# Splitting POOL's weight subtraction into two halves, and PE's wait with it

## The reference, cut to what matters

```
h = h + hgrn2_mixer(rmsnorm(h, ...), w_q, w_f, w_i, w_g, g_norm, w_o, lb)
h = h + sq_relu_mlp(rmsnorm(h, ...), w_up, w_down)      # square(relu(x @ up)) @ down
k_nope, k_rope, v = shared_mla_kv(h, ...)
h = h + mla_mixer(rmsnorm(h, ...), ...)                 # softmax attention
...
x = x + merged @ w_out ; x = x + (silu(gate) * val) @ w_ffn_down
```

## Time and profile before

| | |
|---|---|
| median of 3 runs | 2708.05 us (2705.83 to 2711.03) |
| the profiled execution, its own time | 2706.62 us |
| its span, first to last instruction | 2704.7 us |
| PE busy | 2563.7 us (95%) |
| POOL busy | 1135.5 us (42%) |
| DVE busy | 1494.2 us (55%) |
| mean granted TensorE clock | 0.984 |

### The profile page before, as it was taken

The page is one execution under the profiler, slowest core; times in us unless marked ns, Lnnn a source line. Parts: engine busy times, 40 slices in busy tenths (PEclk is TensorE's granted clock), DMA queues, the critical chain, the costliest instruction groups (busy, mean ns, idle before and its releaser), DMA issues.

```text
span 2704.7 us, 31079 instructions
## 1 busy us (share of the span) xinstructions
PE 2563.7 (95%) x11716; PEld 2038.7 (75%) x11716; DVE 1494.2 (55%) x2034; ACT 673.1 (25%) x1319; POOL 1135.5 (42%) x764
## 2 busy tenths in 40 slices
PE   8999899999978999999999999999989998899998
PEld 6888688888757768888887677777766667688886
DVE  4764565465666634645657674444445787555511
ACT  2003521021324431200213213333322431222200
POOL 3333255555522125555554353333322224455554
PEclk9999899999989999999999999999999999899999
DMA  6334366565522126656654474454454435456655
GB/s 202 125 110 141 101 192 196 189 197 190 187 78 78 63 79 193 195 188 198 206 188 154 145 240 152 158 166 143 154 192 145 135 111 180 151 191 194 195 188 170
DMA packets 149049, 436.62 MB, mean 161 GB/s; under 512 B 14064, under 2 KB 18352, under 8 KB 148912
## 3 DMA queue, kind: packets, MB, share of 16 engines
q1 hardware_dynamic: 64224, 200.29, 25.0%
q0 software_dynamic: 67584, 201.35, 21.3%
q10 hardware_dynamic: 17104, 33.14, 3.6%
HBM read 417.90 MB, written 16.83 MB: 161 GB/s over the span
## 4 chain that ended last, share of the span: by engine, by line
issue 35%; PE 34%; POOL 24%; DVE 3%; DMA 2%; ACT 1%; DVEq 1%; ACTq 0%; POOLq 0%; SPq 0%
POOL w_lo L471 19%; PE bank L523 9%; PE bank L525 9%; PE bank L526 9%; POOL w_hi L453 5%; PE bank L730 2%; DMA projections<-spill_out 1%; PE bank L1157 1%; PE bank L1166 1%; PE bank L804 1%; PE bank L807 0%; PE bank L806 0%; DMA residual<-x_in 0%; PE bank L1124 0%; DVE next_gained L2376 0%
## 5 line engine op out<-in xcount | busy, mean ns | idle before, releaser
L471 POOL TENSOR_TENSOR w_lo<-w_raw,w_hi 128x1024 fp32r<-128x1024 f32 x376 | 903.0, 2402 | 14.5 <-DMA w_hi<-stream 6.4
L453 POOL DMA_DIRECT2D w_hi<-stream x376 | 226.3, 602 | 1537.1 <-PE bank L523 1349.2
L523 PE MATMUL bank<-x_hi,w_hi 128*128 128x512 f32 x1464 | 588.9, 402 | 27.6 <-POOL w_lo L471 14.7
L525 PE MATMUL bank<-x_lo,w_hi 128*128 128x512 f32 x1464 | 574.3, 392 | 0.0
L526 PE MATMUL bank<-x_hi,w_lo 128*128 128x512 f32 x1464 | 573.8, 392 | 0.0
L523 PEld LDWEIGHTS bank<-x_hi,w_hi 128*128 128x128 f32 x1464 | 277.3, 189 | 113.2 <-issue 40.0
L526 PEld LDWEIGHTS bank<-x_hi,w_lo 128*128 128x128 f32 x1464 | 277.2, 189 | 59.2
L525 PEld LDWEIGHTS bank<-x_lo,w_hi 128*128 128x128 f32 x1464 | 277.7, 190 | 56.0 <-issue 2.4
L2084 DVE TENSOR_TENSOR relu_sq<-relu 128x512 f32<-128x512 f32 x64 | 178.7, 2792 | 94.4 <-ACT relu L1459 94.4
L526 PE MATMUL bank<-hidden_hi,w_lo 128*128 128x512 f32 x512 | 199.2, 389 | 0.0
L525 PE MATMUL bank<-hidden_lo,w_hi 128*128 128x512 f32 x512 | 199.2, 389 | 0.0
(11 more groups left out here) (447 smaller groups left out, 4488.2 us busy)
## 6 DMA issues: line engine op xcount, KB each, us to landing
w_hi<-stream POOLq DMA_DIRECT2D x376, 512.0 KB, 4.8
w_raw<-stream SPq DMA_DIRECT2D x376, 512.0 KB, 3.7
projections<-spill_out ACTq DMA_DIRECT2D x56, 256.0 KB, 2.1
ssm_x<-projections ACTq DMA_DIRECT2D x4, 1024.0 KB, 7.1
gate_tiles<-projections ACTq DMA_DIRECT2D x16, 256.0 KB, 2.8
ssm_z<-projections ACTq DMA_DIRECT2D x16, 256.0 KB, 2.6
residual<-x_in SPq DMA_DIRECT2D x4, 512.0 KB, 10.5
toeplitz_hi<-toeplitz_rows_hi POOLq DMA_DIRECT2D x4, 512.0 KB, 6.4
```

The lines of the kernel that those rows point to most:

```text
L453: e.dma_start(in_slot(whi, t % SLOTS, o), in_stream(o)).then_inc(hi_ready[t % SLOTS], 16)
L471: e.tensor_tensor(wlo[:, s, :], raw[:, s, :], whi[:, s, :].bitcast(F32), ALU.subtract).then_inc(lo_ready, 1)
L523: mm = e.matmul(out, wh, rh, start=first, stop=False)
L525: e.matmul(out, wh, rl, start=False, stop=False)
```

## The change

POOL subtracts each tile in two instructions of 512 columns, blocks 0 to 3 and then blocks 4 to 7, and raises the semaphore after each. The semaphore is counted in halves. PE waits at block 0 for the first half and at block 4 for the second. The signal that frees a slot is still given once a tile. `Reader.tile` now waits for both halves before its first matmul.

```
-        lo_ready = sem("lo_ready")
+        lo_ready = sem("lo_half_ready")
...
-                e.tensor_tensor(wlo[:, s, :], raw[:, s, :], whi[:, s, :].bitcast(F32),
-                                ALU.subtract).then_inc(lo_ready, 1)
+                for half in range(2):
+                    cut = slice(512 * half, 512 * half + 512)
+                    e.tensor_tensor(wlo[:, s, cut], raw[:, s, cut], whi[:, s, cut].bitcast(F32),
+                                    ALU.subtract).then_inc(lo_ready, 1)
...
-                    if b == 0:
-                        tile = pos[0] // BLK
-
-                        e.wait_ge(lo_ready, (tile + 1) if i is None else stride * i + (tile + 1))
-                        self.fresh = True
+                    if b % (BLK // 2) == 0:
+                        half = pos[0] // (BLK // 2)
+
+                        e.wait_ge(lo_ready, (half + 1) if i is None else 2 * stride * i + (half + 1))
+                        self.fresh = self.fresh or b == 0
```

## The result

The changed kernel takes 2719.89 us (median of 20 runs, 2716.33 to 2723.91) and the kernel before, run beside it, 2712.51 us (20 runs, 2705.57 to 2719.86). The ratio is 1.0026, 95% interval [1.0018, 1.0035]: slower by 0.26%, just past the 0.2% that a measurement here can tell. I had forecast 2706.4 us, a ratio of 0.9994, "within 0.2%" as the likeliest and 2714 as the top of the range. The time missed the range. A third of the distance is bad luck with the base: the forecast stood on a median of three runs, 2708.05, and twenty runs of the same kernel gave 2712.51, 4.5 us more. The rest, 9.0 us, is the change itself: forecast 1.6 us faster, measured 7.4 us slower. Three executions on record, one of the kernel before (3577.41 us), one of changed_filled (3731.10) and one of dense_split_filled (5206.77), ran over 30% longer than the others and are left out of every comparison.

A forecast was written before the change was run, and what follows sets the result against it. PE was taken as the bound, busy 95% of the span, so only its 141 us standing still could pay. 2706.62 - 4.7 + 3.0 = 2704.9 profiled, 2706.4 for the runs; the likeliest case's range was 2701 to 2714.

The forecast's parts named there:

- Cost of one half: POOL's subtraction: first half ready after 1.30 us, 1.10 earlier than now; two halves near 2.55.
- e: Extra POOL time of a split tile over a whole subtraction: taken as 0.15 us, between 0 and 0.52.
- f: Fixed part of one POOL subtraction: taken as 0.20 us, between the zero end and DVE's share of 0.33.
- Rival 2: POOL's fixed part is large, so 20 holds each cost more: about 2715 us; chance 0.10 with a reverse shift of holds.
- The late tiles: PE's starts on two latent-stage and three dense-stage tiles come earlier: gains 1.10 + 1.09 and 1.59 us.
- The first tile: At the kernel's start PE begins up to 1.05 us earlier; 0.9 counted as gain.
- PE's added waits: Some 370 new waits at block 4 cost nothing; uncovered, up to 3.7 us.
- POOL's queue: The cast now stands behind two subtractions; POOL's 2.46 us idle in dense stages covers the extra time.
- DVE beside the subtraction: POOL keeps the port through both halves, so 20 DVE holds on PE's path end 0.15 later: 3.0 us lost.
- rival 1: DVE gets in between POOL's halves, shortening holds in attention: 18.2 us gained there, about 2685 us; chance 0.25.
- Each hold costs e: Each of 20 DVE holds on PE's path ends 0.15 us later, 3.0 us in all.
- rival 3: Earlier starts shift attention's subtractions so fewer hold `mla_probs`, up to 1.8 us each: 2702 us or less; chance 0.07.

The follow-up runs named there:

- changed_filled: Changed kernel plus four unread PE matmuls ahead of the wait in each of nine latent-attention stalls: 2711.60 us, ratio 1.0002 to the kernel before.
- dense_split_filled: Kernel before with only dense-stage tiles split, PE waiting by halves, and four unread matmuls in each of nine latent-attention stalls: 2706.66 us, 0.9981.
- waits_filled: Kernel before with PE waiting by halves on a whole subtraction, plus four unread matmuls in each of nine latent-attention stalls: 2710.34 us, 1.0000.
- before_filled: Kernel before plus four unread PE matmuls in each of nine latent-attention stalls: 2708.65 us, 0.9998.
- second_half_after_block4: Changed kernel, but POOL subtracts a tile's second half only once PE has run the previous tile's first block-4 matmul: 2702.45 us, 0.9961 to the kernel before.
- section 5: Changed kernel splitting only dense-stage, attention or four latent-stage tiles, or all but the latent attention's: 1.0016, 1.0020, 0.9991, 1.0018 to the kernel before.
- runs 1 and 2: Kernel before with only PE's waits by halves (2712.37 us, 1.0011), then with only POOL's split and one signal after the second half (2724.07 us, 1.0062).
- split_in_attention_only: Changed kernel splitting only the tiles of the latent attention, sparse attention and state space, others subtracted whole: 2717.03 us, 1.0020 to the kernel before.
- late_tiles_only: Changed kernel splitting only the five tiles PE had waited for behind the first, others subtracted whole: 2710.27 us, 1.0003 to the kernel before.
- split_in_dense_stages: Changed kernel splitting only tiles of the MLPs, latent products and FFN from its fourth tile, others whole: 2714.14 us, 1.0016 to the kernel before.
- quarters: Changed kernel with four subtractions of 256 columns a tile, signals after the second and fourth: 2725.13 us, 1.0055 to the kernel before.

## Why the prediction was wrong, point by point

- **Cost of one half.** Right. Predicted 1.30 for one and 2.55 for two, measured 1.296 and 2.54. So e is 0.14, f 0.19, and the value between zero and the proportional share taken from DVE's rows was a good choice; DVE's 14% itself would have given 0.33. Rival 2, a large fixed part, is out.
- **The late tiles.** Right. The waits for `w_lo` fell to the first tile's. Predicted 1.10 + 1.09 + 1.59 = 3.8; measured from start to start 1.09 and 1.08 in the latent stage, 0.37, 0.92 and 0.65 in the dense ones, 4.1 in all.
- **The first tile.** The gain of 0.9 isn't shown. I counted it because the next subtraction moves forward as well. The first matmul did start 1.41 after POOL's first subtraction instead of 2.48. But the pieces hold DVE's instructions for the first tile too:

```profile
14.50 1.38 POOL L473 TENSOR_TENSOR w_lo<-w_raw,w_hi 128x512 fp32r<-128x512 f32 x1
...
14.66 1.76 DVE L1939 TENSOR_TENSOR x_lo<-x_gained,x_hi 128x512 fp32r<-128x512 f32 x1
...
15.84 1.72 POOL L473 TENSOR_TENSOR w_lo<-w_raw,w_hi 128x512 fp32r<-128x512 f32 x1
...
16.48 0.80 PE L525 MATMUL bank<-x_hi,w_hi 128*128 128x512 f32 x1 [0.43 <-DVE x_lo L1939]
17.07 0.63 PE L527 MATMUL bank<-x_lo,w_hi 128*128 128x512 f32 x1
...
17.76 0.68 DVE L1939 TENSOR_TENSOR x_lo<-x_gained,x_hi 128x512 fp32r<-128x512 f32 x1
...
18.49 0.79 PE L525 MATMUL bank<-x_hi,w_hi 128*128 128x512 f32 x1 [0.37 <-DVE x_lo L1939]
```

  `x_lo` takes 1.76 beside the subtraction and 0.68 without, and PE waits three times, 1.07 in all, where it had waited once for 0.99. On the clock of the span the tile ends 0.9 later than before, but the loads had also landed later: POOL's first subtraction began at 11.10 instead of 9.94. In the nine profiles with the first tile whole PE's 97th matmul starts between 41.3 and 44.1 us, in the eight with it split between 41.5 and 44.0. Neither a gain nor a loss can be told from that.
- **PE's added waits.** Right at nothing: 204.45 us for the same 900 matmuls with and without them. waits_filled differs from before_filled by 0.0002, with intervals of 0.0014 to either side.
- **POOL's queue.** Right. The cast goes out on time; POOL's idle time before it fell from 2.46 to 2.31, by e.
- **DVE beside the subtraction, and rival 1.** Right where it mattered, not everywhere. `relu_sq` measured 3.46 (predicted 3.47), the waits at L1006 21.1 (predicted 21). All 137 DVE instructions of the profiled run that stood held when a first half began stayed held through the second. Of 37 held ones that came during the first half, 29 were held through and eight got in at the seam, as rival 1 has it. The `x_lo` above is one: it ends at 16.42, 0.54 after the first half's end at 15.88, and the second half is stretched to 1.72. All eight had started within 0.26 us of the first half's start; others that did were held, and what decides it is open. With a seam of 0.60 (second_half_after_block4) DVE does get in, and `relu_sq` is 2.23.
- **Each hold costs e.** Right in mechanism: a stall of 1.79 became one of 1.91, 0.12 longer.

```profile
795.84 2.96 DVE L2220 TENSOR_SCALAR mla_probs<-mla_probs,mla_row_inv 128x384 f32<-128x384 f32 x1
...
796.08 2.49 POOL L473 TENSOR_TENSOR w_lo<-w_raw,w_hi 128x512 fp32r<-128x512 f32 x2
...
798.85 0.55 PE L1006 MATMUL bank<-consts,mla_probs 128*128 128x128 f32 x3 [1.91 <-DVE mla_probs L2220]
```

  Nineteen times 0.13 are 2.5 us. The twentieth hold moved to another instruction, which cost 2.0 us (section 5). Together 4.5, where I had 3.0. My rival 3 named such a shift as likely in either direction, put its reverse among the 0.10 for slower, and gave it no price.
- **The step that failed is the sum itself.** "2706.62 - 4.7 + 3.0" adds up only time in which PE stands still, and takes for granted that the 2563.7 us in which PE is busy stay as they are. They grew by 10.3 in the profile. The same step stands at the head of the prediction, "a change pays only in the 141 us in which PE stands still". With the terms as measured, -4.1 for the late tiles and +4.5 for the holds, the change would be +0.4 us, and at equal clock it is +0.8; the changed kernel is 7.4 us slower in the median. The other 7 us go with the clock. The profile of before had the row in it: PEclk 0.97 over the latent attention and behind the second MLP, beside 1.00 in the MLP. I put no price on what the change would do to it.

What is shown: the loss goes with the clock (the tables by mean clock and at equal clock), it comes with POOL's split and not with PE's waits (runs 1 and 2), and fills in the stalls of the latent attention bring the median clock and the time of the changed kernel back to those of the kernel before.

What is only argued: that the 0.12 us by which those stalls are longer is what sends PE to the lower clock more often. Several runs fit it badly. split_in_attention_only has the longer stalls and kept a median of 0.982. With the latent attention subtracted whole, the changed kernel recovered 2 us, while the fills recovered 6, and its median clock stayed at 0.979. late_tiles_only and split_in_dense_stages left attention alone and still ran at a median of 0.980. quarters made the stalls longer again and left the median clock where it was, and second_half_after_block4 made PE's waits 9 us shorter and ran at 0.980. Most low stretches lie at the same places in the two profiles (near 288, 298, 318, 752, 772, 1476, 1555 and 2320 to 2330 us), some longer after the change; others, such as one in the first stage, come in some executions and not in others, and the kernel before itself spreads from 2705 to 2720. With 11 or 12 runs a median clock is not known to better than about 0.001, which is 2 us. So how much of each stage's clock the split takes, and by what step, stays open, and so does why less idle time came with a lower clock in three kernels.

## What to carry to other kernels

When PE is the bound, its busy time is no constant. Read PEclk stage by stage, and where it is below 1.00 give each stall that a change makes longer a second price, that of the clock: here terms that add up to 0.4 us went with 10.3 us more of busy time in the profiled run. How large that price is can't be read off in advance: shorter stalls came with a lower clock too. Cutting an instruction of POOL in two seldom lets DVE in if the second piece follows at once (8 of 174 held instructions here); put the second piece behind a signal that comes a little later, and DVE gets in at no cost to a POOL that has slack. A hold that grows by 0.13 us can also move to another instruction and cost 2 us, so compare the waits stage by stage and not only the one that was priced. A change worth 0.1% should be compared at equal mean clock, since the run-to-run scatter of the clock alone is worth 0.5%.

## What the runs showed of the hardware that was not expected

- A drain on POOL between two subtractions that do not depend on each other left 2.24 us of idle time at the place shown and 2.61 in the median, about as much as a whole subtraction takes (2.40).
- A POOL subtraction of 256 columns takes 0.739 in the median (0.762 on average) beside 1.296 for 512 and 2.40 for 1024: some 0.2 us fixed. The Trainium skill (GPSIMD Engine Reference, "Elementwise — side-by-side cycle accounting") led by its 2048-column figure to an estimate of 0.31 fixed; the measured pair, 2.54 against 2.40 with 0.05 of overlap, gives 0.19.
- Two POOL subtractions of 1.30 us back to back mostly hold DVE as one does: `relu_sq` took 3.46 beside them, and 166 of 174 DVE instructions were held through both. The Trainium skill (SBUF — State Buffer, "Who interferes with whom") has the lock held for an instruction; in the changed kernel it passed on at the seam eight times, and with the gap of 0.60 in second_half_after_block4 at most places (`relu_sq` at 2.2 us in 53 of 64).
- Thirty-six more matmuls in PE's stalls (9 x 4) cost no time that the runs can tell (0.9998, and -1.6 us at equal clock).
